# Third attention: exponentials scaled by reciprocal sums in place of turned reciprocals, and turns and values at other distances

## The reference, cut to what matters

```python
sc = einsum('bqhd,bkhd->bhqk', q_blk, k) * scale      # 128 queries at a time
sc = where(k_pos[None, :] <= q_pos[:, None], sc, -inf)
p = softmax(sc, axis=-1)
out = einsum('bhqk,bkhd->bqhd', p, v)
...
y = concatenate([tok, mem_out], axis=-1) * silu(gate)
```

## Time and profile before

| | |
|---|---|
| median of 3 runs | 3104.64 us (3103.66 to 3106.8) |
| profiled execution, its own time | 3105.86 us |
| its span | 3104.1 us |
| TensorE matmuls busy | 3032.0 us, 98% |
| VectorE busy | 1915.0 us, 62% |
| ScalarE busy | 1373.9 us, 44% |
| GpSimd busy | 717.3 us, 23% |
| third attention in the span | about 2404 to 2684 us |

### The profile page before, as it was taken

The page is one execution under the profiler, slowest core; times in us unless marked ns, Lnnn a source line. Parts: engine busy times, 40 slices in busy tenths (PEclk is TensorE's granted clock), DMA queues, the critical chain, the costliest instruction groups (busy, mean ns, idle before and its releaser), DMA issues.

```text
span 3104.1 us, 50426 instructions
## 1 busy us (share of the span) xinstructions
PE 3032.0 (98%) x18252; PEld 2572.1 (83%) x18252; DVE 1915.0 (62%) x3747; ACT 1373.9 (44%) x2723; POOL 717.3 (23%) x926
## 2 busy tenths in 40 slices
PE   7999999999999999999999999999999999999999
PEld 7988888999999788888788888888977777687677
DVE  6657675263543655675888887876353657753675
ACT  5446565444444444332333333455433556522552
POOL 3424334366643000001111111001101111022230
PEclk9999999999999999999999999999999999999999
DMA  5110011122211333652233225644100000221012
GB/s 200 43 37 30 21 35 50 31 66 72 72 56 35 138 127 102 227 189 90 72 107 109 106 102 191 210 150 141 51 29 22 16 28 29 96 82 58 28 62 102
DMA packets 96808, 264.84 MB, mean 85 GB/s; under 512 B 19568, under 2 KB 24176, under 8 KB 84144
## 3 DMA queue, kind: packets, MB, share of 16 engines
q1 hardware_dynamic: 96560, 261.61, 24.4%
HBM read 200.69 MB, written 60.62 MB: 84 GB/s over the span
## 4 chain that ended last, share of the span: by engine, by line
PE 85%; DVE 6%; ACT 3%; POOL 2%; issue 2%; DMA 1%; SPq 0%; DVEq 0%; POOLq 0%; ACTq 0%
PE ps L2847 66%; PE ps L2890 7%; PE ps L2898 3%; PE ps L2854 2%; PE ps L2905 2%; PE ps L2921 2%; PE ps L2913 1%; POOL gs L3451 1%; PE ps L2924 1%; PE ps L2941 1%; POOL stats L3459 1%; POOL wlo L3447 1%; DVE qk L3224 0%; DVE hlo L3193 0%; DVE wlo L3116 0%
## 5 line engine op out<-in xcount | busy, mean ns | idle before, releaser
L2847 PE MATMUL ps<-whi,hhi 128*128 128x256 f32 (+2 forms) x1920 | 579.4, 302 | 2.6 <-DVE hlo L3193 1.3
L2847 PE MATMUL ps<-whi,hlo 128*128 128x256 f32 (+2 forms) x1920 | 562.7, 293 | 0.0
L2847 PE MATMUL ps<-wlo,hhi 128*128 128x256 f32 (+2 forms) x1920 | 561.8, 293 | 0.0
L2847 PEld LDWEIGHTS ps<-whi,hhi 128*128 128x128 f32 x1920 | 368.1, 192 | 12.5 <-issue 4.4
L2847 PEld LDWEIGHTS ps<-wlo,hhi 128*128 128x128 f32 x1920 | 368.6, 192 | 7.6 <-issue 0.2
L2847 PEld LDWEIGHTS ps<-whi,hlo 128*128 128x128 f32 x1920 | 368.1, 192 | 7.6
L3456 POOL TENSOR_SCALAR stats<-stats 128x2 f32<-128x2 f32 (+2 forms) x230 | 58.5, 254 | 1142.7 <-ACT xsf L2955 490.0
L3445 POOL CAST whi<-raw 128x512 fp32r<-128x512 f32 (+2 forms) x180 | 113.6, 631 | 832.8 <-PE ps L2847 805.5
L2847 PE MATMUL ps<-hhi,whi 128*128 128x512 f32 x640 | 255.6, 399 | 0.2 <-DVE hlo L3116 0.2
L2847 PE MATMUL ps<-hhi,wlo 128*128 128x512 f32 x640 | 249.9, 390 | 0.0
L2847 PE MATMUL ps<-hlo,whi 128*128 128x512 f32 x640 | 249.2, 389 | 0.0
(11 more groups left out here) (783 smaller groups left out, 7443.0 us busy)
## 6 DMA issues: line engine op xcount, KB each, us to landing
raw<-in_W SPq DMA_DIRECT2D x60, 1024.0 KB, 4.9
scratch_fs<-fo SPq DMA_DIRECT2D x77, 256.0 KB, 2.0
scr<-scratch_gates SPq DMA_DIRECT2D x48, 256.0 KB, 3.1
scratch_gates<-go SPq DMA_DIRECT2D x46, 256.0 KB, 2.5
wd<-in_WD SPq DMA_DIRECT2D x44, 256.0 KB, 3.5
wf0b<-in_WF SPq DMA_DIRECT2D x10, 1024.0 KB, 5.1
wf1b<-in_WF SPq DMA_DIRECT2D x10, 1024.0 KB, 5.2
scratch_x<-x SPq DMA_DIRECT2D x16, 512.0 KB, 3.1
```

The lines of the kernel that those rows point to most:

```text
L2847: x = e.matmul(r.out, a, b, start=(r.start and m == 0), stop=(r.stop and m == n - 1), skip_group_check=r.joined)
```

## The change

For the third attention alone the exponentials themselves are scaled by the reciprocal of their row sum, before they are turned. `combine` emits `e_norm` for each unit in step i + 1. For an even unit VectorE takes the reciprocal and ScalarE multiplies the whole row of mE in place; for an odd unit VectorE does both. The turns wait for that product. The turn of mO, the spread copy and the first gate product are gone. Turns come three steps behind the scores and not two, values one step behind the turns and not two, so that the sum of both distances stays four. There are four buffers mE, two mPT and no mO.

```diff
@@ combine
-                if self.paired and u.mate:
+                if self.normed:
+                    u.norm_by_act = not u.mate
+                    u.inverse = signal("e_norm")
+                    u.normed = signal("exp") if u.norm_by_act else u.inverse
+                    u.ecols = u.E[:, 0:128 * u.nblk]
+                    emit("e_norm", u)
+                    u.e_ready = [u.normed]
+                elif self.paired and u.mate:
@@ buffers and steps
-        mE = ... 2 + [rest("mE2", [T], F, 76 * KB)]
+        mE = ... 2 + [rest(f"mE{2 + i}", [T], F, (76 + 4 * i) * KB) for i in range(2)]
-        mPT = ... 2 + [rest("mPT2", [T], F, 80 * KB)]
+        mPT = ... 2
-        attM = Att(..., [x[:, :] for x in mO], SB2, OB2, paired=True)
+        attM = Att(..., [], SB2, OB2, paired=True, normed=True)
-        m_steps = attM.steps(us, lag_t=2, fill=fills_m(), fill_n=1, lag_v=2)
+        m_steps = attM.steps(us, lag_t=3, fill=fills_m(), fill_n=1, lag_v=1)
@@ TensorE, pair_value
-                    w.wait_ge(*r.spread)
-                    e.transpose(r.v_place.ps[:, 128:256], r.o, ident[:, :]).then_inc(r.v_place.full[0], 1)
+                    if r.scaled:
+                        x.then_inc(r.v_place.full[0], 1)
+                    else:
+                        w.wait_ge(*r.spread)
+                        e.transpose(r.v_place.ps[:, 128:256], r.o, ident[:, :]).then_inc(r.v_place.full[0], 1)
@@ ScalarE
+                elif kind == "e_norm" and r.norm_by_act:
+                    w.wait_ge(*w.last)
+                    w.wait_ge(*r.inverse)
+                    e.activation(r.ecols, r.ecols, ACT.Copy, scale=r.dens[0]).then_inc(w.sig(r.normed), 1)
@@ VectorE
+                elif kind == "e_norm":
+                    w.wait_each(r.exps)
+                    w.wait_ge(*w.last)
+                    if r.norm_by_act:
+                        e.reciprocal(r.dens[0], r.dens[0]).then_inc(w.sig(r.inverse), 1)
+                    else:
+                        inner(lambda: e.reciprocal(r.dens[0], r.dens[0]))
+                        w.wait_ge(*w.last)
+                        e.tensor_scalar(r.ecols, r.ecols, r.dens[0], None, ALU.mult).then_inc(w.sig(r.normed), 1)
@@ VectorE, pair_mul
-                    inner(lambda: e.tensor_tensor(r.gate, r.v_place.ps[:, 128:256], r.gate, ALU.mult))
+                    if not r.scaled:
+                        inner(lambda: e.tensor_tensor(r.gate, r.v_place.ps[:, 128:256], r.gate, ALU.mult))
```

More of the change, by code:

```diff
@@ L654, in build, with __init__ @@
         class Att:
-            def __init__(self, E, PT, os_, sb, ob, dve_turns=True, together=False, paired=False, by_feature=False, between=False):
-                self.by_feature, self.between = by_feature, between
+            def __init__(self, E, PT, os_, sb, ob, dve_turns=True, together=False, paired=False, by_feature=False, between=False, normed=False):
+                self.by_feature, self.between, self.normed = by_feature, between, normed
                 self.E, self.PT, self.O, self.sb, self.ob = Slots(E), Slots(PT), Slots(os_), sb, ob
@@ L707, in scored @@
                         x_.den = u.kept[1]
-                    elif not self.paired:
+                    elif not self.paired or self.normed:
                         x_.den = stat(1)
@@ L760, in pair_values @@
                 u.v_ready = flat(u.vready, u.v_at() if u.v_at else None, u.mate.pt_read, u.pt_read)
+                u.scaled = self.normed
                 emit("pair_value", u)
@@ L764, in pair_values @@
                     self.PT.free[x.pi] = [u.v_place.full]
-                self.O.free[u.oi] = [u.v_place.full]
+                if not self.normed:
+                    self.O.free[u.oi] = [u.v_place.full]
             def values(self, u):
@@ L2402, in build @@
         mV = [inh(f"mV{i}", [8, 128], F, (38 + 4 * i) * KB) for i in range(2)] + [rest("mV2", [8, 128], F, 72 * KB)]
-        mE = [inh(f"mE{i}", [T], F, (46 + 4 * i) * KB) for i in range(2)] + [rest("mE2", [T], F, 76 * KB)]
+        mE = [inh(f"mE{i}", [T], F, (46 + 4 * i) * KB) for i in range(2)] + [rest(f"mE{2 + i}", [T], F, (76 + 4 * i) * KB) for i in range(2)]
         gE = [rest(f"gE{i}", [256], F, (16 + i) * KB) for i in range(4)]
@@ L2408, in build @@
         nPT = [inh(f"nPT{i}", [256], F, (54 + i) * KB) for i in range(4)]
-        mPT = [inh(f"mPT{i}", [T], F, (54 + 4 * i) * KB) for i in range(2)] + [rest("mPT2", [T], F, 80 * KB)]
+        mPT = [inh(f"mPT{i}", [T], F, (54 + 4 * i) * KB) for i in range(2)]
         mO = [inh(f"mO{i}", [128], F, 62 * KB + 512 * i) for i in range(2)]
@@ L2539, in build @@
         n_done[:] = [mem_us[-1].v_full, mem_us[-1].fin, mem_us[-1].s_full]
-        attM = Att([x[:, :] for x in mE], [x[:, :] for x in mPT], [x[:, :] for x in mO], SB2, OB2, paired=True)
+        attM = Att([x[:, :] for x in mE], [x[:, :] for x in mPT], [], SB2, OB2, paired=True, normed=True)
         for s_ in (attM.E, attM.PT, attM.O):
```

## The result

The changed kernel takes 3163.14 us in the median of four runs (3160.98 to 3167.89), the kernel before, run beside it, 3104.15 us (3103.13 to 3106.8): ratio 1.0192 [1.018, 1.0204], 59.0 us slower. The profiled execution was its longest, 3167.89 us with a span of 3166.1.

What follows compares the result with a forecast made beforehand. TensorE was taken to set the pace almost everywhere, with VectorE's order mattering in the last part. 3104.6 plus 40 (late copies, removed turns counted in) plus 15 (clock falls) gave 3159 us; range 3120 to 3182.

Steps and rivals of the forecast that it cites:

- The late copies: Third attention: value matmuls wait for VectorE's copy of turned exponentials; 40 us slower, 8.2 us of removed turns counted in.
- The shifts of the sum: How much later value matmuls start, by key blocks per pair: 12.0, 9.6, 7.0, 2.3, 1.0, 4.5, last two 3 us.
- The tails of 2.23 and 1.89 us: Time from VectorE's reciprocal through scaling, evacuation and copy to the value matmuls, for pairs of eight and seven key blocks.
- rival d: Half of the waits are made up as VectorE and ScalarE catch up: +15 to +25 us, 3125; chance 0.08.
- The gain: TensorE loses the turned reciprocals, 0.17 us each, 48 times: 8.2 us saved.
- The clock: TensorE's granted clock falls after long new waits: 10 events of 1.5 us, 15 us, ends 0 and 27.
- rival (b): The same waits at the values without falls of the clock: +40 us, 3145; chance 0.20.
- (c): Clock falls in nearly every wait, or scaling runs one column a cycle, with GpSimd against it: 72 us, 3177; chance 0.15.
- The scalings' own length: VectorE scales the odd unit's exponentials at two columns a cycle: 0.75 us for 1024 columns, 0.69 for 896.
- ScalarE's scaling at nothing: ScalarE's scaling of even units, about 37 us over 48 units, costs nothing; up to 0.3 us a pair without cover.
- VectorE beside GpSimd: VectorE scalings meeting GpSimd's weight splits lose some 0.5 us on at most 15 pairs: 0 to 5 us, taken as 0.

Runs made afterwards that it cites:

- none22: `scale_only` with neither reciprocals nor scaling, so the output is not divided by the row sums: 3098.7 us, ratio 0.9981.
- kept_busy: The changed kernel with 15 to 22 unused identity turns on TensorE ahead of the value matmuls in twelve pairs: 3153.16 us, ratio 1.0158.
- scale_only: The changed kernel at the old distances (turns two behind scores, values two behind turns), three buffers mE and three mPT: 3129.79 us, ratio 1.0083.
- lag32: The changed kernel with turns three steps behind scores, values two behind turns, four buffers mE and three mPT: 3123.57 us, ratio 1.0064.
- lag32_late: `lag32` with reciprocal and scaling emitted two steps after the scores instead of one: 3133.01 us, ratio 1.0092.

## Why the prediction was right

The forecast was 3159 us, the runs gave 3163.14. By its own steps:

- **The late copies.** The sum had 40 us, which with the 8.2 us of gain counted in is 48.2 us of waits. Measured are 52.2 less the 3.9 of before: 48.3. By n from 8 to 1 the waits are 14.1, 10.2, 7.3, 4.1, 2.7, 7.1, 2.3 and 4.4 us. Before, n of 4 to 1 already had 0.7, 2.1, 0.5 and 0.5, so that what was added is 14.1, 10.2, 7.3, 4.1, 1.9, 5.0 and, for the last two together, 5.6. The shifts of the sum, each six with the 1.0 us of gain counted in taken out again, are 13.0, 10.6, 8.0, 3.3, 2.0, 5.5 and 5.0: each is right to some 1 us. The tails of 2.23 and 1.89 us were met exactly. For n of 2 and 1 the prediction had no rows and put 3 us on them; that this fits is luck. That part of these waits could be made up (rival d) fell: V to the next R takes 6.85 us where the clock holds, 7.03 before.
- **Shown by a change of it.** With only distances and buffers changed, +43.1 us; with the odd unit's scaling out of the tail, 28 us back, 16 of them waits at V. The waits at V are thus the cause and not an echo. No run has three buffers mPT at distances 3 and 1; in the timeline above VectorE's copy starts right behind the evacuation, 0.05 us after it, and so did not wait for a buffer.
- **The gain.** 8.2 us of turns removed was too much: `none22` has 5.8, the spread copy and gate product included. In its trace the scores do start 0.17 us sooner behind V, in 47 of 48 pairs. But in 46 of them the second instruction of these scores then comes 0.10 us later behind the first (0.53 instead of 0.43 us for 512 columns), 4.6 us in all. The changed kernel shows it too: scores right behind the value matmuls are recorded with 1.12 us, those behind the turned reciprocals with 1.02.

```profile
2546.59 1.12 PE L2899 MATMUL ps<-mkT,mqT 96*128 96x512 f32 x2
```

The term was therefore read one start too early; why the second instruction comes later is open.
- **The clock.** Forecast ten falls of 1.5 us, 15 us; seen ten of 1.7 and one of 3.4, 20.5 us more than before in the profiled execution. The prediction took its ten from two falls and no rule, so that the count is luck in part. The profiled execution had the lowest clock of the four (0.990, the others 0.991 to 0.993), and it is 4.75 us above the median. If all of these are put down to the clock, some 15.7 us are left. `kept_busy` returned 10.0 us, with 202 more turns on TensorE and two of the new falls left. So rival (b) is out by a run, and (c) was wrong in the count: of 15 waits from 1.79 to 2.96 us four had no fall behind them.
- **Closing the sum.** For the profiled executions 48.3 + 20.5 - 5.8 = 63.0 us, and the stage grew by 63.1. For the medians 48.3 + 15.7 - 5.8 = 58.2 us, measured 59.0; there the clock's term is what the 4.75 us leave, and is not measured by itself. The forecast had 48.2 + 15 - 8.2 = 55, low by 4 us, 2.4 of them the gain that was put too high.
- **The scalings' own length.** Forecast 0.75, 0.69 and 0.62 us on VectorE for 1024, 896 and 768 columns, and 1.15 on ScalarE; the groups say 754, 686, 654 and 1149 ns:

```profile
L3268 DVE TENSOR_SCALAR mE<-mE,stats 128x1024 f32<-128x1024 f32 x6 | 4.5, 754 | 0.2
L3268 DVE TENSOR_SCALAR mE<-mE,stats 128x896 f32<-128x896 f32 x6 | 4.1, 686 | 0.2
L3268 DVE TENSOR_SCALAR mE<-mE,stats 128x768 f32<-128x768 f32 x6 | 3.9, 654 | 0.2
...
L3268 DVE TENSOR_SCALAR mE<-mE,stats 128x256 f32<-128x256 f32 x6 | 2.5, 411 | 0.2
...
L3014 ACT ACTIVATE mE<-mE,stats 128x1024 f32<-128x1024 f32 x6 | 6.9, 1149 | 2.9 <-DVE stats L3264 2.8
```

The 0.067 us for each 128 columns, as taken from the rows of before, hold up to 1024. The Trainium skill (VectorE: DVE Perf Modes, SBUF-source operations) has 58 cycles plus half the columns, 0.59 us by the prediction's working; the trace does not agree, 0.754. The same section adds that its formula is too low and that the fixed term it measured is about 150 cycles, which gives an estimate of 0.69 us; the 0.06 us that are left are what the prediction put on the per-partition operand.
- **ScalarE's scaling at nothing** held in the changed kernel (V waits for ScalarE's copy 3.1 us, where it had not been named), but only because the third step hid it. As a statement about the scaling it was wrong, and the expectations of `scale_only`, `lag32` and `lag32_late`, which carried it over, fell by 27 to 35 us. I had looked for what is queued behind the scaling on ScalarE and not for who waits for its result.
- **VectorE beside GpSimd** was taken at 0, with 5 us as its end. The mean of 411 ns for 256 columns above, between 322 for 128 and 422 for 384, hides a scaling of 0.69 us and others of 0.35:

```profile
2516.23 0.58 POOL L3471 CAST whi<-raw 128x480 fp32r<-128x480 f32 x1
2516.27 0.69 DVE L3268 TENSOR_SCALAR mE<-mE,stats 128x256 f32<-128x256 f32 x1
2516.89 1.20 POOL L3473 TENSOR_TENSOR wlo<-raw,whi 128x480 fp32r<-128x480 f32 x1
```

It began beside a weight split of GpSimd and ended 0.07 us into the next. Three of the 48 scalings are like that (0.69 for 0.35, 0.49 for 0.29, 0.82 for 0.62), 0.7 us in all. The rule of the Trainium skill that the prediction weighed (SBUF — State Buffer, "two separate sides") would have them held so; these three agree with it, but three others that began beside a split kept their length (0.75 for 1024 columns at 2413.21 and 2527.64, 0.35 for 256 at 2627.58), which the rule does not give; times on GpSimd are rough. The price here is small either way.

What stays open: what the distances 3 and 2 cost by themselves, why some waits of over 2 us are followed by a fall of the clock and others are not; and a scaling on GpSimd, which wasn't tried.

## What to carry to other kernels

On engines that work in a written order, price a moved step as the serial tail from the last event that it waits for to its consumer, through everything that then stands between on that engine; where the tail ends at the engine that sets the pace, it is paid in full, though no engine is full. Ask two questions of each added operation, not one: what is queued behind it, and who waits for its result; here the second was worth 25 us of waits in `scale_only`. And bound a gain by a kernel that leaves the thing out altogether before giving anything for it: here the floor was 5.8 us below, and the best arrangement paid 13.

## What I had not expected of the hardware

A long wait of TensorE does not always cost its clock: behind V's wait of 2.48 us at 2536.17 the grant stays at 1.00, behind one just as long at 2647.68, and behind waits of 2.02 to 2.10 us elsewhere, it falls to 0.50. When it falls, it costs the same nearly each time, 1.70 to 1.72 us of grant in ten of eleven cases, and 1.66 us on the chain. And where the third attention loses most, no engine's busy time bounds it any more: with work taken off TensorE, its busy share of the last 85 us is 73%, where it was nearly full before.
